# First stage on x without its norms, other order of the norms, forms on GpSimd, a normalisation on ScalarE

## The reference, cut to what matters

```python
h = rms_norm(x, norm_g)                    # x * rsqrt(mean(x*x) + EPS) * g, per token
proj = h @ w_in                            # q, k, v, ..., u, v_sgu, ...
# branch C (spatial gating), with v = v_sgu:
v = layer_norm(v, ln_g, ln_b)              # per token: (v - mean) * rsqrt(var + EPS) * g + b
mixed = einsum('gij,bnjgc->bnigc', w, v)   # mixes the 128 positions of a chunk
# branch A (attention) first does, per head:
q = apply_rope(rms_norm(q, q_norm_g), cos, sin)
k = apply_rope(rms_norm(k, k_norm_g), cos, sin)
```

## Time and profile before

| | |
|---|---|
| median of 3 runs | 2114.64 us (2114.01 to 2114.9) |
| the profiled execution's own time | 2112.07 us |
| its span, first to last instruction | 2110.3 us |
| mean granted TensorE clock | 0.997 |
| busy share PE / DVE / ACT / POOL | 99% / 61% / 39% / 61% |
| DMA, mean over the span | 93 GB/s |

### The profile page before, as it was taken

One profiled execution on the slowest core, in us unless ns is written; L12 is line 12 of the kernel. 1 busy time (PEld: TensorE's weight loads), 2 busy tenths in 40 slices (PEclk: granted clock), 3 DMA queues, 4 the chain that ended last, 5 costly groups with the idle time before them and its releaser, 6 DMA issues.

```text
span 2110.3 us, 27107 instructions
## 1 busy us (share of the span) xinstructions
PE 2081.9 (99%) x9676; PEld 1711.9 (81%) x9676; DVE 1292.5 (61%) x1510; ACT 823.1 (39%) x1571; POOL 1286.9 (61%) x987
## 2 busy tenths in 40 slices
PE   6999999999999999999999999999999999999999
PEld 5888877788887888888888888778888878888887
DVE  7875544688988635335378845447888875452331
ACT  5434555233223335324344245443332243343331
POOL 5557544677678667654455664447766866675543
PEclk9999999999999999999999999999999999999999
DMA  5322232313341344314543132323134313434163
GB/s 190 87 64 96 66 120 81 120 51 76 81 96 44 71 84 81 135 55 155 156 129 97 55 100 86 100 95 99 51 80 91 76 41 80 90 70 140 50 199 100
DMA packets 114277, 197.24 MB, mean 93 GB/s; under 512 B 12256, under 2 KB 21216, under 8 KB 114144
## 3 DMA queue, kind: packets, MB, share of 16 engines
q1 hardware_dynamic: 96864, 164.70, 25.4%
q0 software_dynamic: 9216, 16.78, 6.0%
q10 hardware_dynamic: 8064, 14.03, 1.8%
HBM read 153.52 MB, written 41.94 MB: 93 GB/s over the span
## 4 chain that ended last, share of the span: by engine, by line
PE 95%; DVE 3%; ACT 1%; issue 0%; DVEq 0%; DMA 0%; SPq 0%; ACTq 0%
PE acc L616 79%; PE acc L664 6%; PE aux L664 4%; PE aux L736 1%; PE aux L755 1%; PE aux L746 1%; DVE pt L1280 1%; PE aux L699 1%; DVE pool L1273 0%; PE aux L766 0%; PE aux L712 0%; PE aux L773 0%; DVE blo L1276 0%; PE acc L805 0%; ACT prob L1065 0%
## 5 line engine op out<-in xcount | busy, mean ns | idle before, releaser
L541 POOL TENSOR_TENSOR wlo<-raw,whi 128x512 fp32r<-128x512 f32 x464 | 633.3, 1366 | 560.3 <-ACT whi L870 559.4
L616 PE MATMUL acc<-fhi,whi 128*128 128x512 f32 x2048 | 804.7, 393 | 0.0
L616 PE MATMUL acc<-fhi,wlo 128*128 128x512 f32 x2048 | 797.2, 389 | 0.0
L616 PE MATMUL acc<-flo,whi 128*128 128x512 f32 x2048 | 797.0, 389 | 0.0
L870 ACT ACTIVATE whi<-raw 128x512 fp32r<-128x512 f32 x464 | 290.8, 627 | 525.7 <-PE acc L616 398.1
L616 PEld LDWEIGHTS acc<-fhi,whi 128*128 128x128 f32 x2048 | 384.7, 188 | 83.3 <-issue 2.7
L616 PEld LDWEIGHTS acc<-flo,whi 128*128 128x128 f32 x2048 | 384.6, 188 | 80.9 <-issue 2.3
L616 PEld LDWEIGHTS acc<-fhi,wlo 128*128 128x128 f32 x2048 | 384.5, 188 | 80.4
L541 POOL TENSOR_TENSOR wlo<-wsum,whi 128x512 fp32r<-128x512 f32 x192 | 269.2, 1402 | 180.6 <-ACT whi L870 180.5
L1280 DVE SCALAR_TENSOR_TENSOR aux<-conv,allp,aux 128x1024 f32<-128x1024 f32 x232 | 299.0, 1289 | 20.4 <-issue 0.9
L616 PE MATMUL acc<-bhi,whi 128*128 128x512 f32 x512 | 201.7, 394 | 0.0
(11 more groups left out here) (182 smaller groups left out, 2349.7 us busy)
## 6 DMA issues: line engine op xcount, KB each, us to landing
raw<-wstream SPq DMA_DIRECT2D x464, 256.0 KB, 2.7
md<-prev POOLq DMA_DIRECT2D x64, 256.0 KB, 4.3
x<-x SPq DMA_DIRECT2D x32, 256.0 KB, 4.9
md<-prev SPq DMA_DIRECT2D x32, 256.0 KB, 3.6
out<-x ACTq DMA_DIRECT2D x32, 256.0 KB, 2.2
mx<-md SPq DMA_DIRECT2D x24, 256.0 KB, 4.8
qd<-qst ACTq DMA_DIRECT2D x16, 256.0 KB, 2.2
qs<-qd SPq DMA_DIRECT2D x16, 256.0 KB, 2.8
```

Source lines behind the costliest of these rows:

```text
L541: nc.gpsimd.tensor_tensor(wlo[:, f % SLOTS, :], src, whi[:, f % SLOTS, :].bitcast(F32), ALU.subtract).then_inc(lo_made, 1)
L616: mm = nc.tensor.matmul(dst, w, m[:, kt0 + k, cols], start=first and k == 0 and n == 0, stop=last and k == UK - 1 and n == 2, skip_group_c ...
```

## The change

1. **The first stage on x.** VS0 of layer 0 multiplies the weights by x times g, not by h. The high part is made by ScalarE from x directly (`x_rounded`, scale g), the rest by VectorE (`x_rest`), into slots that are free then (`X_SLOT`). The layer norm behind VS0 divides the missing factor per token out again, but for EPS; so VectorE multiplies the variance twice by the norm factor `rms` before the root and the result once after it, in instructions of a few elements.
2. **Order of norms.** Layer 0 normalises its second half first (`turn`). The squares of the second half are added on VectorE, those of the first on GpSimd, between low parts (`SQUARES_AT`). Sums and spread of the second half stand after steps 4 and 5 of VS0, those of the first half after steps 0 and 3 of VS1; ScalarE copies each spread from PSUM to SBUF (`take_spread`). VS1 waits per step for its operands; the first half's h is only needed for Q0.
3. **Loads.** SP interleaves x's blocks, the column constants and the weights; each block of the first half has a semaphore of its own. 30 warm-up matmuls at once, not 16 behind the first squares.
4. **Forms on GpSimd.** The eight 128x1024 forms of each layer go from VectorE to GpSimd, one behind a low part each, at (Q1,5) to (Q0,0) in layer 0 and (VS1,4) to (Q1,3) in layer 1. One of them changes its sign, and `sum_x` its sign with it. The `form_rest` instructions move to later places on VectorE, among the statistics and after `normalise`; `square_q` waits for some of them.
5. **vs normalised on ScalarE.** Eight `activation`s with scale and bias (`normal_vs`) between the highs of KV1, with a small `shift` from VectorE, in place of eight VectorE instructions.

```diff
-WARMUP = 16
+WARMUP = 30
+        FORM_AT = ([("Q1", 5), ("Q1", 6), ("Q1", 7), ("KV1", 0), ("KV1", 1), ("KV1", 2), ("KV1", 3), ("Q0", 0)],
+                   [("VS1", 4), ("VS1", 5), ("VS1", 6), ("VS1", 7), ("Q1", 0), ("Q1", 1), ("Q1", 2), ("Q1", 3)])
+        SQUARES_AT = {3: (1, 2), 4: (3,), 5: (4,), 6: (5, 6), 7: (7,)}
...
+            load_x(0, 0)
+            sp.dma_start(allp[:], cols).then_inc(cols_loaded, 16)
+            load_unit(0, "VS0", 0)
+            for k in range(1, KT):
+                load_x(k, 0)
+                if k % 2 == 0:
+                    load_unit(0, "VS0", k // 2)
+            for k in range(KT):
+                load_x(k, 1)
+                if k in (1, 3):
+                    load_unit(0, "VS0", 4 + k // 2)
+            sp.dma_start(ident[:], ident_in).then_inc(ident_loaded, 16)
+            load_unit(0, "VS0", 6)
             load_rows(sp, 0)
+            load_unit(0, "VS0", 7)
...
+            def form(L, n):
+                at = slice(n % 2 * 2, n % 2 * 2 + 2)
+                b11, b12, b22, b21 = (q[:, at, :] for q in (x11, x12, x22, x21))
+                if n == 0:
+                    pool.wait_ge(h_ready, (L + 1) * 2 * KT)
+                if n >= 4:
+                    pool.wait_ge(form_made, 8 * L + n - 1)
+                if n < 2:
+                    op = nc.gpsimd.tensor_tensor(b11, b11, b12, ALU.subtract)
...
+                        if (name, k) in FORM_AT[L]:
+                            form(L, FORM_AT[L].index((name, k)))
+                        for e in SQUARES_AT.get(k, ()) if (L, name) == (0, "VS0") else ():
+                            pool.wait_ge(xsq_stored, e + 1)
+                            if e > 1:
+                                pool.wait_ge(xsq_pooled, e - 1)
+                            add(sumsq[:, 0:HALF], sumsq[:, 0:HALF], sqs[:, e, :], xsq_pooled)
...
+                    if (L, name) == (0, "VS0"):
+                        pe.wait_ge(x_ready, k + 1)
+                    elif (L, name) == (0, "VS1"):
+                        pe.wait_ge(h_ready, k + 1)
+                    elif (L, name, k) == (0, "Q0", 0):
+                        pe.wait_ge(h_ready, 2 * KT)
...
-                at = (1, 2, 3) if L else (2, 3, 4)
+                at = (1, 2, 3) if L else (4, 5, 6)
-                token_major(L, "VS1", 8, 1, aux)
+                token_major(L, "VS1", 8, 1, aux, None if L else {0: lambda: token_sums(0, 0), 3: lambda: spread(0, 0)})
...
+            def normal_vs(L, tiles):
+                act.wait_ge(vs_scales, L + 1)
+                for t in tiles:
+                    nc.scalar.activation(vs[:, t, :], vs[:, t, :], ACT.Identity, bias=shift[:, t:t + 1],
+                                         scale=rstd[:, 1, t:t + 1]).then_inc(vs_ready, 1)
             def square_q(L, n):
                 tile = (4, 6, 0, 2)[n]
+                act.wait_ge(form_ready, 8 * L + (2 if n < 2 else 4))
...
+            act.wait_ge(cols_loaded, 16)
             for k in range(KT):
+                x_rounded(k)
+                if k % 2 == 0:
+                    high(k // 2)
+                elif k < KT - 1:
+                    x_squared(k // 2, x_block(k // 2, 0))
+            for k in range(KT):
+                act.wait_ge(x_loaded[KT + k // 2], 16 * 2)
+                x_squared(KT + k, x_block(k, 1))
+                if k in (1, 4, 7):
+                    next_high(0, "VS0", k // 3)
+            for k in range(3, KT):
+                x_squared(k, x_block(k, 0))
+            next_high(0, "VS0", 3)
+            rms_stage(1)
...
                 for k in range(8):
                     next_high(L, "Q1", k)
+                    if not L and k >= 2:
+                        form_rounded(L, k - 2)
+                    if k == 6:
                         act.wait_ge(sgu_var, L + 1)
...
+                if L:
+                    h_all(2 * L + 1, {KT - 1: row_bias})
+                else:
+                    h_all(1, {2: row_bias, KT: lambda: rms_diagonals(0)})
+                    h_all(0, {})
-                for n in range(8):
-                    dve.drain()
-                    form(L, n)
-                    if n >= 2:
-                        form_rest(L, n - 2)
...
                 op.then_inc(sgu_var, 1)
+                form_rest(L, 2)
+                form_rest(L, 3)
                 dve.wait_ge(sgu_root, L + 1)
                 nc.vector.reciprocal(rstd[:, 1, :], rstd[:, 0, :])
...
+                form_rest(L, 0)
+                form_rest(L, 1)
                 mean_squares(L, 0)
                 mean_squares(L, 1)
                 normalise(L, 0)
                 normalise(L, 1)
+                form_rest(L, 4)
+                form_rest(L, 5)
                 rotate(L, 0)
```

More of the change, by code:

```diff
@@ L209, in hybrid_block @@
         sq = place("sq", [P, 2, HALF], F32, at_z + 4096)
+        spreads = place("spreads", [P, 2, HALF], F32, at_z + 12288)
         vs = place("vs", [P, TT, W], F32, at_t)
@@ L1141, in _ @@
                     next_high(L, "KV1", k)
+                    if k < 3:
+                        normal_vs(L, range(4 * k - 4, 4 * k))
                 square_k(L, 1)
@@ L1410, in sum_x @@
                 dve.wait_ge(step_done, stepped(L, st, i, "p6"))
-                add(x_, x_, BANK_AP["b"]).then_inc(taken["b"], 1)
+                sub(x_, x_, BANK_AP["b"]).then_inc(taken["b"], 1)
             def sum_v(L, st, i):
@@ L1665, in _ @@
                     op = nc.vector.bn_aggr(mv[:, t, :], stv[:, t, :])
+                if not L:
+                    for _ in range(2):
+                        dve.drain()
+                        op = mul(mv[:, 0:TT // 2, 1], mv[:, 0:TT // 2, 1], rms[:])
                 op.then_inc(sgu_var, 1)
+                form_rest(L, 2)
+                form_rest(L, 3)
                 dve.wait_ge(sgu_root, L + 1)
```

205 lines of the change are left out of this document (110 added, 95 removed).

## The result

The changed kernel takes 2117.49 us (median of 14 runs, 2116.46 to 2121.16); the kernel before took 2114.82 beside it (14 runs). The ratio is 1.0016, 95% interval 1.0009 to 1.0023 (the two medians alone would give 1.0013): slower by 0.16%, and outside the predicted range of 2099.5 to 2113.5. One of the 14 runs of the kernel before took 2243.02 us, in a slow state of the chip, and the ratio leaves it out; the others took 2113.23 to 2115.96. The profiled execution took 2116.48 us with a span of 2114.7, against 2112.07 and 2110.3 before: 4.4 us more in the span.

A forecast was written before the change was run, and what follows sets the result against it. It took TensorE's waits, mostly in the first 51 us, and its unbroken matmuls afterwards as the bound. Terms -15.0 + 4.2 + 0.6 + 1.4 = -8.8 us gave 2105.8 against the median 2114.64, range 2099.5 to 2113.5.

The forecast's parts named there:

- The forms: Both layers' forms on GpSimd: 2.4 us each, low parts and q's squares late, losses of 4.2, 0.6 and 1.4 us.
- What costs nothing: Moving vs normalisations and forms off VectorE, small products and added loads: covered, since TensorE did not wait for VectorE.
- 0.5 us for each of four rests: First layer ahead of Q0: contention with GpSimd lengthens four two-input VectorE rests, 2.0 us in all.
- The start: First layer up to Q1: VS0 on unnormalised x begins at 7.8, Q1 at 59.3, gaining 15.0 us.
- wait for low 5: In VS0 of the first layer: TensorE idles from 22.5 to 24.7 behind GpSimd's square sum, a gap of 2.2 us.
- Ahead of Q0: First layer: Q0 stalls 4.2 us, 2.2 from late squares of q and 2.0 from contention; bounds 0 and 9.
- The term of 0.6 behind Q0 (sgu_mix): First layer: k's normalisation comes late ahead of the first sgu_mix, costing 0.6 us; bounds 0 and 2.2.
- Second layer: Eight forms on GpSimd delay low parts until Q1 there waits, costing 1.4 us; bounds 0 and 9.
- the clock falls again: Rival, chance 0.10: idle in VS0 and ahead of Q0 is followed by the half-level clock, 3.8 us, giving 2110.4.
- The port case: Rival, chance 0.17: port held for whole instructions, rests cost 1.2 each, forms about 2.8; loss 14, giving 2113.6.
- The slower case: Rival, chance 0.08: a form on GpSimd takes 3.5 us through VectorE's traffic; 6.6 us slower, 2121.2.
- a form's mean below 3.0: Sign on GpSimd: forms' mean 2.4 to 2.8 expected; above 3.0 us would show the prediction wrong.

The follow-up runs named there:

- e3: Changed kernel with the first layer's eight GpSimd forms cut to one column of 512 each, results not the reference's: 2104.59 us, ratio 0.9956 to the kernel before.
- e1: Changed kernel without the first layer's eight rope-table products on VectorE, one fill instead, results not the reference's: 2116.32 us, ratio 1.0009 to the kernel before.
- e4: Changed kernel with both layers' forms back on VectorE, in a row ahead of the rope tables: 2113.9 us, ratio 0.9996 to the kernel before.
- e11: Changed kernel with the eight normalisations of vs back on VectorE, ahead of rests 0 and 1: 2125.02 us, ratio 1.005 to the kernel before.
- e8: Changed kernel with GpSimd's seven additions of squares in the start cut to two columns, results not the reference's: 2113.54 us, ratio 0.9998 to the kernel before.
- e7: Changed kernel with only the second layer's forms back on VectorE: 2115.48 us, ratio 1.0005 to the kernel before.
- e15: e14 with U's first sum ahead of two rotations and the second between them on VectorE: 2110.77 us, ratio 0.9978 to the kernel before.
- e9: Changed kernel, all forms on VectorE, first layer's split four ahead of q's normalisations, four behind, tables after: 2114.52 us, ratio 1.0 to the kernel before.
- e13: e9 with the gate's products (oc) taken ahead of the rotations in the first layer: 2111.35 us, ratio 0.998 to the kernel before.
- e14: e13 with k's reduction and normalisation ahead of two rotations on VectorE: 2117.1 us, ratio 1.0012 to the kernel before.

## Why the prediction was wrong

**The step that failed** is in "The forms": "The eight 128x1024 forms go from VectorE, which had room, to GpSimd", with its twin under "What costs nothing", that the move "frees an engine that TensorE did not wait for". VectorE had 1.5 us to spare between Q1 and Q0. The last rest of h ends there at 69.6 in place of 50.5, so that from 69.6 to Q0 VectorE has one queue without a gap: tables, statistics of vs, rests, reductions, normalisations. The sum priced that queue at its old durations and added 0.5 us for each of four rests. What was left out is VectorE's side of the collision for everything else with two operands in SBUF: tables 14.9 instead of 5.1, the two products of mv 1.60 instead of 0.40, the product of rstd 0.95 instead of 0.16, shift 2.25 instead of 0.17 (e3's rows are the undisturbed ones). Those are 13.9 us against the 2.0 that stood there. That e1 gained 1 us and e3 12.9 shows that it is not the tables as such: with the forms on GpSimd its own queue is as late as VectorE's. That e4, without a form on GpSimd, starts Q0 at 106.85 shows that the forms had no room on VectorE either, and e11 that the queue there is what Q0 waits for.

**The sum, term by term** (profiled executions):
- The start: 10.0 in place of 15.0 (the steps of VS1 as the prediction gives them end at 59.1, not 59.3, a slip of 0.2). VS0 began at 9.78 (7.8 forecast), because 60 warm-up records took 8.9 us. The wait for low 5 is there, as predicted, but its square sum came at 24.79 instead of 22.1, which the prediction had named as a sign of being wrong: ScalarE waited 2.2 us for VectorE's sums through two buffers, and these took 8.16 for seven beside GpSimd's. That is 2.6 of the 5. The rest came behind it, from scalings at 1.6 to 1.8 and token sums that waited for ScalarE's copies (1.6 us, where 1.0 was forecast). e8 puts the sums' whole part at 4.7.
- Ahead of Q0: Q0 starts 10.6 us after it could have (64.2 + 33.3 = 97.5), where 4.2 was forecast. 2.5 of that is a wait for wlo and 6.3 the wait for rotq; the rest is low clock. The squares of q ended 33.8 us after Q1's start, where 31.15 and a share of the 2.0 for contention were forecast, and the reductions, forecast right behind them, began 4.8 us later.
- The term of 0.6 behind Q0 (sgu_mix) did not occur, but 1.6 us of clock did: Q0's first four steps took 12.51 instead of 10.91.
- Second layer: 1.4 forecast, and Q1 there is 1.4 longer (23.15 for 21.76). The whole layer loses 1.0 (its VS0 starts 3.4 us later than before, its end is 4.4 later); e7's median gives 2.0.
- Not in the sum: 1.3 us more in the rest of the first layer. It is 1.4 gained, with a wait of 1.1 for prob near 371 that is gone, and 2.6 lost around the pooled matmuls. There the wait is the same, but the clock is at the half level behind it, and four matmuls took 3.78 where they took 1.98. The kernel before and e4 show the full level there; why it differs is not known.

Together, with 1.4 for Q0 and KV0 as the stage starts show it (U is 2.1 late where Q0 was 0.7 late), -10.0 + 10.7 + 1.4 + 1.3 + 1.0 = +4.4, the difference of the spans.

**The clock, by rows.** Windows of the changed kernel (PE, PEld, DVE, ACT, POOL, PEclk, DMA, GB/s):

```profile
99.00:100.00 1.00, 1.00 (x7) 1.00 (x6) 1.00 (x2) 0.00 (x0) 1.00 (x2) 0.50 0.25 94
...
108.00:109.00 1.00, 0.87 (x2) 0.77 (x3) 1.00 (x2) 1.00 (x3) 0.00 (x0) 0.50 0.57 147
109.00:110.00 1.00, 1.00 (x3) 0.72 (x3) 1.00 (x2) 1.00 (x3) 0.49 (x1) 0.50 0.33 115
...
112.00:113.00 1.00, 1.00 (x7) 0.81 (x5) 1.00 (x3) 1.00 (x3) 0.15 (x1) 1.00 0.48 129
...
688.00:689.00 1.00, 1.00 (x3) 0.38 (x2) 0.54 (x1) 0.00 (x0) 0.60 (x1) 0.50 0.61 234
```

PEclk 0.50 is 1.2 GHz, 1.00 is 2.4. TensorE had waited 6.3 us when Q0 began at 108.13, at the lower level, and it is back at the full one by 112. Behind the wait of 2.5 in KV1 the same shows at 99, and behind the pooled gap at 688. So the rival "the clock falls again" was right for Q0, at 1.6 us. In VS0 it was wrong, as the sum had it: behind the wait of 1.7 us that ended at 27.33 the granted clock stayed at 1.00.

**The rivals.** The port case (0.17, 2113.6), that the port is held for whole instructions, named the right mechanism and was too small, since it priced rests and forms only and no other work of VectorE; the forms' mean was 2.58 where it had 2.8. The slower case (0.08) had the wrong one: no form reached 3.5; they took 2.37 to 3.45, and 2.37 to 2.40 where VectorE did not delay them, as forecast. The sign that would have told the two apart, a form's mean below 3.0, was met, and the kernel was slower all the same: the price was on the other engine.

**What was right.** The wait for low 5, the undelayed form of 2.4, the price of the second layer's forms, and that Q0 waits for rotq and the squares of q for ScalarE's rounding of form 5 (95.02 to 96.08, then the squares). Of the signs named, VS0's start (9.78 for 7 to 9), Q1's (64.2 for 58 to 61) and the length of Q0's wait (6.3 for 3 to 5) missed. One reading was wrong from the outset: "No wait of the second layer is in the earlier trace rows" overlooks that one of the two 3.6 us waits before pooled matmuls is in the second layer; it is there after the change as well and cancels.

**Page and trace.** The Trainium skill ("SBUF — State Buffer", Who interferes with whom) says that a VectorE instruction with two SBUF inputs contends with a GpSimd instruction that reads SBUF, and that the one issued first keeps the shared ports until it is through. The rows agree on both sides: a table of 0.41 takes 1.5 or 2.6 and ends 0.3 us behind the low part or form ahead of it, and a form of 2.4 took 3.45 where a rest had started 0.02 us before it. The prediction had applied that rule to four rests alone; applied to every two-input operation from 69.6 to Q0 it would have pointed at the loss.

**What stays open.** How e8's 4.7 us divide; why the clock fell at the pooled matmuls; how e3's 12.9 us divide between the forms' own time and their collisions; and whether U's last 5.9 us in e15 yield to order. A version with GpSimd's forms and e15's order wasn't tried.

## What to carry to other kernels

Before work goes to GpSimd, write down what VectorE does in that stretch and price each of its operations with two operands in SBUF at a wait for the GpSimd instruction under way, the smallest first, since 0.17 us became 2.25: here moving 16.8 us away gave nothing back. Read an engine's room from the stretch where the work will lie after the change, not from its share of the span or from TensorE's waits. When a wait is cured and the time stays, look for the next one by the same view: e9, e13, e14 and e15 are one queue, and only its order made a ratio of 1.0000 into 0.9980, 1.0012 and 0.9978.

## What the hardware showed that was not expected

- The wait is per instruction, and the two engines take turns. Beside GpSimd a VectorE product of 128x256 took 1.51 or 2.62 (0.41 alone), one of 128x512 1.77 or 2.88 (0.68 alone), one of 128x8 2.25 (0.17 alone), each until a little behind the end of the GpSimd instruction under way.
- The same scaling of x took 0.74 on average in the kernel before, with one operand in PSUM (mean 737 ns of 13, lines of VectorE from 20 to 175), and 1158 ns in the mean of 16 when the operand had been copied to SBUF:

```profile
L1280 DVE SCALAR_TENSOR_TENSOR x<-x,allp,aux 128x512 f32<-128x512 f32 x13 | 9.4, 737 | 0.0
```

```profile
L1381 DVE SCALAR_TENSOR_TENSOR x<-x,allp,spreads 128x512 f32<-128x512 f32 x16 | 18.3, 1158 | 1.5 <-ACT spreads L930 1.5
```

- A queue that stands still makes its neighbour fast: with GpSimd waiting, four products of 128x256 took 1.43 us (e13), with GpSimd at work 5.89 (e14).
